# Split weights 16 bytes into their allocation, everything behind them 32 bytes later

## The reference

```python
for layer in range(2):
    h = rms_norm(x, norm_mix[layer])
    p = h @ w_in[layer]                  # 1024 x 2816, then 1024 x 3072
    x = x + mixers(p) @ w_out[layer]     # gMLP and attention, attention and short convolution
    h = rms_norm(x, norm_ffn[layer])
    if layer == 0:
        x = x + (silu(h @ wg) * (h @ wu)) @ wd              # width 2816
    else:                                                   # 8 experts of width 3584, top 2 gated
        for e in range(8):
            x = x + gate[..., e:e+1] * ((silu(h @ wg[e]) * (h @ wu[e])) @ wd[e])
```

## Time and profile before

| what | value |
|---|---|
| median of 3 runs | 1383.89 us (1383.48 to 1384.07) |
| the profiled execution, its own time | 1383.98 us |
| its span, first to last instruction | 1382.2 us |
| TensorE (matmul) busy | 1367.8 us, 99% |
| VectorE busy | 1194.1 us, 86% |
| ScalarE busy | 1026.2 us, 74% |
| mean granted TensorE clock | 0.999 |

### The profile page before, as it was taken

One profiled execution on the slowest core, in us unless ns is written; L12 is line 12 of the kernel. 1 busy time (PEld: TensorE's weight loads), 2 busy tenths in 40 slices (PEclk: granted clock), 3 DMA queues, 4 the chain that ended last, 5 costly groups with the idle time before them and its releaser, 6 DMA issues.

```text
span 1382.2 us, 20276 instructions
## 1 busy us (share of the span) xinstructions
PE 1367.8 (99%) x6985; PEld 1152.5 (83%) x6985; DVE 1194.1 (86%) x1517; ACT 1026.2 (74%) x1262; POOL 86.1 (6%) x67
## 2 busy tenths in 40 slices
PE   9999999999999999999999999999999999999998
PEld 7778999988988788888888888888888888888886
DVE  5876555568959999999999999999999999999998
ACT  5666444456758788888888888888888788888877
POOL 1020000000220000000100100010010001001000
PEclk9999999999999999999999999999999999999999
DMA  9944543643658999999999999999999999999980
GB/s 346 357 152 152 183 153 122 222 144 122 245 183 321 363 375 353 388 391 379 359 393 380 336 395 396 382 356 388 382 355 394 386 377 358 386 379 344 394 332 30
DMA packets 183760, 430.28 MB, mean 311 GB/s; under 512 B 5449, under 2 KB 13301, under 8 KB 183712
## 3 DMA queue, kind: packets, MB, share of 16 engines
q1 hardware_dynamic: 181408, 423.86, 82.9%
q0 software_dynamic: 2304, 5.78, 1.9%
HBM read 425.09 MB, written 7.34 MB: 313 GB/s over the span
## 4 chain that ended last, share of the span: by engine, by line
PE 92%; DVE 5%; ACT 1%; issue 1%; DMA 0%; SPq 0%; DVEq 0%; ACTq 0%
PE psum L723 29%; PE psum L725 29%; PE psum L724 29%; PE psum L1310 2%; DVE w_lo L411 1%; DVE w_lo L393 1%; PE psum L1291 0%; DVE act_lo L1877 0%; PE psum L755 0%; PE psum L856 0%; DVE probs L2075 0%; PE psum L997 0%; PE psum L888 0%; DMA const<-const_f 0%; ACT act_hi L1392 0%
## 5 line engine op out<-in xcount | busy, mean ns | idle before, releaser
L411 DVE TENSOR_TENSOR w_lo<-raw_ring,w_hi 128x1024 fp32r<-128x1024 f32 x674 | 812.4, 1224 | 48.2 <-ACT w_hi L406 4.0
L406 ACT ACTIVATE w_hi<-raw_ring 128x1024 fp32r<-128x1024 f32 x675 | 715.2, 1063 | 169.0 <-PE psum L725 168.5
L723 PE MATMUL psum<-w_hi,xg_hi 128*128 128x512 f32 x896 | 353.4, 394 | 1.1 <-DVE w_lo L411 1.0
L725 PE MATMUL psum<-w_hi,xg_lo 128*128 128x512 f32 x896 | 349.3, 390 | 0.0
L724 PE MATMUL psum<-w_lo,xg_hi 128*128 128x512 f32 x896 | 348.9, 389 | 0.0
L393 DVE TENSOR_TENSOR w_lo<-raw_ring,w_hi 128x1024 fp32r<-128x1024 f32 x124 | 151.5, 1229 | 80.2 <-ACT w_hi L385 79.3
L385 ACT ACTIVATE w_hi<-raw_ring 128x1024 fp32r<-128x1024 f32 x124 | 130.0, 1058 | 96.4 <-PE psum L725 96.2
L725 PEld LDWEIGHTS psum<-w_hi,xg_lo 128*128 128x128 f32 x896 | 168.2, 188 | 35.7
L723 PEld LDWEIGHTS psum<-w_hi,xg_hi 128*128 128x128 f32 x896 | 168.3, 188 | 34.9 <-issue 1.5
L724 PEld LDWEIGHTS psum<-w_lo,xg_hi 128*128 128x128 f32 x896 | 168.4, 188 | 33.6
L723 PE MATMUL psum<-w_hi,moe_hT_hi 128*128 128x512 f32 x448 | 176.0, 393 | 0.1
(11 more groups left out here) (272 smaller groups left out, 1279.3 us busy)
## 6 DMA issues: line engine op xcount, KB each, us to landing
raw_ring<-in_moe_w_gate SPq DMA_DIRECT2D x56, 2048.0 KB, 10.2
raw_ring<-in_moe_w_up SPq DMA_DIRECT2D x56, 2048.0 KB, 10.5
raw_ring<-in_moe_w_down SPq DMA_DIRECT2D x56, 2048.0 KB, 10.4
raw_ring<-in_ffn_w_gate SPq DMA_DIRECT2D x5, 2048.0 KB, 7.9
raw_ring<-in_ffn_w_up SPq DMA_DIRECT2D x5, 2048.0 KB, 9.2
raw_ring<-in_ffn_w_down SPq DMA_DIRECT2D x5, 2048.0 KB, 10.2
raw_ring<-in_w_in_ab SPq DMA_DIRECT2D x4, 2048.0 KB, 16.5
raw_ring<-in_w_in_cd SPq DMA_DIRECT2D x4, 2048.0 KB, 8.1
```

Source lines behind the costliest of these rows:

```text
L406: act.activation(wh[:, v % SPLITS, :], moe_raw(i, q), ACT.Copy).then_inc(hi_ready, 1)
L411: dve.tensor_tensor(wl[:, v % SPLITS, :], moe_raw(i, q), wh[:, v % SPLITS, :].bitcast(F32), ALU.subtract).then_inc(lo_ready, 1)
L723: pe.matmul(out_, sh, mh_, start=start, stop=False)
L725: return pe.matmul(out_, sl, mh_, start=False, stop=stop)
```

## The change

The two split buffers become one allocation with 32 bytes more. The views on it begin 4 floats, 16 bytes, after its start, and `w_lo` follows `w_hi` directly. All that is placed after it, the activations' region included, moves by 32 bytes. No instruction is added, removed or reordered. Only addresses differ.

```diff
-PHASE = 32
+PHASE, LINE = 32, 4
...
-        wh = keep("w_hi", [SPLITS, UNIT], F32R)
-        wl = keep("w_lo", [SPLITS, UNIT], F32R)
+        split = keep("w_split", [2 * SPLITS * UNIT + 2 * LINE], F32R)
+        wh = split[:, LINE:LINE + SPLITS * UNIT].rearrange("p (s f) -> p s f", s=SPLITS)
+        wl = split[:, LINE + SPLITS * UNIT:LINE + 2 * SPLITS * UNIT].rearrange("p (s f) -> p s f", s=SPLITS)
```

## The result

The changed kernel takes 1418.88 us, median of 6 runs (1418.33 to 1419.16), against 1383.70 for the kernel before on the same chip (6 runs, 1383.32 to 1384.45): a ratio of 1.0253, 95% interval 1.0243 to 1.0264. It is 35.2 us slower, where 1350 was forecast. The rival "the meeting gets worse" had 1418. The profiled execution took 1418.82 us, its span is 1417.0 (before: 1382.2), its mean granted clock 1.00. The helper's lines are one further down: L724, L725 and L726 stand for L723 to L725, L407 for L406, L412 for L411.

The account below looks back on a forecast made before the run. TensorE was taken to bound the kernel. From 1383.98 us, 33.8 us less by rows and 0 for columns and other engines gave 1350.2, forecast as 1350 us, 2.4% less, range 1325 to 1400.

Parts of the forecast that it names:

- the meeting gets worse: Rival, fp32r matmuls by rows: a whole step more, 1418 us and up, 0.18 with VectorE; quarter step, 1392, 0.10.
- What bounds the kernel: Whole kernel: TensorE sets the pace, VectorE follows 41 us behind in 800, and transfers have room.
- the fee of 13.3 ns: Each fp32r matmul, with the next weight load under it, pays 13.3 ns in which no column moves.
- the by-rows term: 5064 fp32r matmuls with activations stationary: each 6.67 ns less, 33.8 us less in all.
- What spoke for a gain: Plain float32 matmul L782, operands 32 bytes apart on the raster, pays near zero; half speed or that offset could explain it.
- By columns: 1008 fp32r matmuls of the reverse roles: 0 taken, with 6.7 us to either side.
- nothing changes: Rival, all fp32r matmuls: the 13.3 ns are fixed or the streams settle again; 1383.9 us, chance 0.30.
- its whole step: Slow rival by rows: one raster step, 6.67 ns, more on 5064 matmuls, 33.8 us more.
- Cover: Expert layer, 800 us: TensorE still leads after the forecast gain; VectorE would cap a larger one near 41 us.
- The raster of 6.67 ns: Guess that two TensorE streams take turns on 64 bytes, 16 columns; intervals are whole multiples of 6.67 ns.

Follow-up runs that it names:

- TensorE alone: Kernels that leave out the whole computation: only matmuls on TensorE, at many pairs of operand starts, no other engine beside them; 525.80 us for the first.
- 0 / 0: Stationary / moving start in bytes past a common raster: the kernel before by rows, 1383.70 us; 226.7 ns at 512 columns with TensorE alone.
- the table: Kernel with TensorE alone, all 16 pairs of stationary and moving starts 0, 16, 32, 48 bytes plus larger distances, 120 matmuls per pair; 1104.08 us.
- 0 / 32: Stationary operand at 0, moving at 32 bytes, run only with TensorE alone: 233.3 ns at 512 columns.
- 32 / 0: Kernel before with the activations' region 32 bytes later, weights at 0: 1408.21 us, ratio 1.0177.
- 32 / 32: Kernel before with every tensor 32 bytes later: 1383.80 us, ratio 1.0000.
- 16 / 0: Kernel before with the activations' region alone 16 bytes further: 1405.05 us, ratio 1.0155.
- 32 / 16: The changed kernel's pair by rows: stationary start 32, moving 16 bytes past a common raster; 1418.88 us, ratio 1.0253.
- 16 / 16: Changed kernel with the activations' region also 16 bytes past a multiple of 32: 1402.44 us, ratio 1.0137.
- a pair that was 64 bytes off: Changed kernel with weights at 32 and activations at 80 bytes, where 16 was meant: 1410.78 us, ratio 1.0197.
- 120 / 0: Stationary operand at 120, moving at 0 bytes, with TensorE alone: 226.7 ns at 512 columns.
- 48 / 16: Stationary operand at 48, moving at 16 bytes, with TensorE alone: 226.7 ns at 512 columns.
- 0 / 192: 256-column pair from the kernel before with activations in part of layer 0 64 bytes earlier, region 256 bytes later: 1381.69 us, ratio 0.9982.

## Why the prediction was wrong

- **What bounds the kernel: right.** TensorE sets the end before and after, its price is to be read from starts, and the fee of 13.3 ns over one column per cycle is real. With TensorE alone 0 / 0 has the same 226.7 ns, and bf16 in the same order has 215.8, 2.5 ns over 213.3.
- **That the fee depends on how the two operands lie to each other: right,** shown by the table. It was the condition for anything to happen.
- **The step that failed is the sign of the by-rows term:** "I take a step less, 6.7 ns, midway between all and nothing". There was no row for it. The fee grew, by (1156.6 - 1120.2) / 4881 = 7.5 ns on the mean of an interval, 36.4 us in all against the forecast's 33.8 less. Size and count were near; the direction was not. The earlier trace rows was read as evidence that the fee can vary, and that is what it is; but each variation that it shows is upwards. 226.7 was the lowest interval at which a stream of 512-column fp32r matmuls settled in the trace before, and of more than 60 pairs tried since none settles lower. A state to which a stream returns after each disturbance, from above, is better evidence for a floor than for a middle. It is no proof: the changed kernel's tiles return from above to 233.3 or 236.7, and the same pair has 226.7 as well. That 226.7 is the floor rests on the tables.
- **What spoke for a gain, L782, was misread.** It pays no such fee, but the distance of 32 bytes isn't the reason: plain float32 has 215.8 ns at all distances tried. Whether it is the slower rate at which it takes its columns, or something that goes with it, wasn't tested apart. The prediction named both reasons and then gave weight to the wrong one.
- **By columns: 0 taken, within 6.7 us; -1.3 measured.** Right, and the small sign is real: blocks of the SwiGLU settle at 120 or at 117.3.
- **Rival "nothing changes": refuted.** The Trainium skill's page "SBUF — State Buffer", section "Who interferes with whom", has TensorE read through two independent ports and never wait. By that rule the time would have stayed; it is 35.2 us more with the same instructions and other addresses, so here the measurement decides. The runs don't count ports. They show that at 512 columns 0 / 32 and 32 / 0 cost 6.7 ns where 0 / 0 and 32 / 32 cost nothing more, so what one stream pays isn't independent of where the other begins.
- **Rival "the meeting gets worse": this is what happened, at the price of its whole step,** 6.67 x 5064 = 33.8, 1418. That the sum meets the measurement so closely is luck: tiles rose by 6.7 or by 10 ns, two groups not at all, and the intervals behind transposes, high before, by less. Its reason, that 16 bytes of lead bring the load into the line that the moving stream wants next, isn't shown. By it 16 / 0 would be the same as 32 / 16, and 16 / 16 free; both are wrong by 13 us or more.
- **Cover and other engines: right where it could be seen.** L412 kept 1224 ns, L407 1063. That VectorE would cap a gain was never put to use.
- **The raster of 6.67 ns:** settled intervals are 226.7, 230.0, 233.3 and 236.7, and 113.3, 116.7 and 120, so steps of 3.3 ns, half of it. Some pairs have means between them (231.6, 232.3). The numbers allow a raster and don't show what makes it.

What is shown: the added cost lies in the intervals of fp32r matmuls, each with a weight load of its own, comes with other starts of the two operands and nothing else changed, is there with TensorE alone, and isn't there in bf16 or plain float32 at the distances tried. What stays open: whether an fp32r matmul without a weight load under it would pay (none was run), which part of the read path makes it, why both starts count and not only their distance (16 / 16 against 32 / 32), and by what the matmuls ahead choose between the intervals of a pair; the number of separating matmuls is the only thing about them that was varied on purpose.

## What to carry to other kernels

In a dense stream of fp32r matmuls of 512 columns, place stationary and moving operands at the same start modulo 256 bytes, both on multiples of 32. That was the floor here whatever stood ahead, and being off it costs up to 10 ns on a matmul; 7.5 on the mean were 2.5% of this kernel. At 256 columns the same placement gave 120 ns, among the slowest, so the longest stream decides. Before a change of addresses is forecast as a gain, TensorE alone with a table of offsets tells the sign in one run, at the very places that the kernel uses: a pair that was 64 bytes off cost 27 us here. The size it tells only roughly, since some pairs have two or three intervals.

## What the runs showed of the hardware

- fp32r has a fee of its own. Over one column per cycle at 2.4 GHz a 512-column matmul pays 13.3 ns at best and 23.3 at worst, a 256-column one from 6.7 (at a distance of 64 bytes) to 13.3 and more. bf16 pays 2.5 (215.8 and, for 256 columns, 109.2 ns), plain float32 of 256 columns, at half the rate, 2.5 too (215.8). The Trainium skill's page "TensorE: Matmul & The Clock Gate", section "Wait — 56ns, not 53.3ns?", gives N / 2.4 GHz and some 2.5 ns for a warm matmul; these runs agree for bf16 (215.8 and 109.2 ns) and not for fp32r, and plain float32 has the same 2.5 ns over twice N / 2.4 GHz.
- The best distance depends on the length that moves: at 512 columns 0 (226.7 ns; 120 / 0 and 48 / 16 have it too), at 256 columns 64 bytes (113.3 or 117.8 ns against 120).
- A shorter weight load doesn't lower the fee at 512 columns (231.7 ns with 32 weight columns against 226.7 with 128) and does at 256 (113.3 against 120.0).
- The stream has a memory. 32 / 16 settles at 226.7, 233.3 or 236.7 ns (the first in the kernel only), 16 / 0 at 226.7 or 233.3, and 0 / 192 (256 columns) at 113.3 or 117.8, for the rest of its stretch, 48 to 120 matmuls. For 32 / 16 and 0 / 192 the number of matmuls ahead was shown to choose.
